# A decoder stack in one program: mod vectors spread over more steps, a first block interleaved with its norm, and a second norm scale taken from block sums

## Time and profile before

| what | value |
|---|---|
| median of 3 runs (lowest to highest) | 1957.84 us (1957.07 to 1960.55) |
| profiled execution | 1955.04 us |
| its span | 1953.4 us |
| mean granted clock of TensorE | 0.983 |
| PE busy | 1845.5 us, 94% |
| DVE busy | 1427.5 us, 73% |
| ACT busy | 902.8 us, 46% |
| POOL busy | 118.3 us, 6% |
| transfers | 424.80 MB, mean 217 GB/s |

### The profile page before, as it was taken

One profiled execution on the slowest core, in us unless ns is written; L12 is line 12 of the kernel. 1 busy time (PEld: TensorE's weight loads), 2 busy tenths in 40 slices (PEclk: granted clock), 3 DMA queues, 4 the chain that ended last, 5 costly groups with the idle time before them and its releaser, 6 DMA issues.

```text
span 1953.4 us, 29752 instructions
## 1 busy us (share of the span) xinstructions
PE 1845.5 (94%) x11620; PEld 1664.0 (85%) x11620; DVE 1427.5 (73%) x1613; ACT 902.8 (46%) x1204; POOL 118.3 (6%) x217
## 2 busy tenths in 40 slices
PE   5999999999999999999999979998999997999997
PEld 5999978789889988988998767776888787999976
DVE  4699996777778887888788967643667666786754
ACT  4444456454434444444444465422556445444442
POOL 0100000001110000000000000000111000000000
PEclk9999999999999999999999989998999998999998
DMA  6855445858888787767877654544444583777652
GB/s 227 285 195 193 161 154 203 280 188 275 314 311 276 241 270 257 252 213 266 257 249 281 231 214 141 200 140 151 162 153 137 204 285 110 242 234 261 212 186 87
DMA packets 185319, 424.80 MB, mean 217 GB/s; under 512 B 8192, under 2 KB 8576, under 8 KB 183680
## 3 DMA queue, kind: packets, MB, share of 16 engines
q1 hardware_dynamic: 157568, 322.69, 48.4%
q0 software_dynamic: 27648, 100.68, 15.6%
HBM read 419.14 MB, written 4.19 MB: 217 GB/s over the span
## 4 chain that ended last, share of the span: by engine, by line
PE 72%; DVE 14%; DMA 6%; ACT 4%; issue 3%; SPq 0%; POOLq 0%; DVEq 0%; ACTq 0%; POOL 0%
PE acc L1622 11%; PE acc L1623 11%; PE acc L1624 11%; PE acc L1609 11%; PE acc L1611 11%; PE acc L1610 11%; DVE w_lo L956 4%; DMA mod_raw<-in_od_mod_w 3%; DMA mod_raw<-in_ev_mod_w 2%; DVE mod_sum L995 2%; DVE mod_sum L1118 2%; PE aux L1658 2%; PE aux L1870 1%; ACT w_hi L482 1%; DVE scratch L1244 1%
## 5 line engine op out<-in xcount | busy, mean ns | idle before, releaser
L482 ACT ACTIVATE w_hi<-raw 128x1024 fp32r<-128x1024 f32 x552 | 575.4, 1057 | 673.1 <-PE acc L1611 331.5
L956 DVE TENSOR_TENSOR w_lo<-raw,w_hi 128x1024 fp32r<-128x1024 f32 x552 | 665.3, 1223 | 273.7 <-ACT w_hi L482 272.7
L1609 PE MATMUL acc<-a_hi,w_hi 128*128 128x256 f32 x2304 | 659.3, 286 | 15.4 <-DVE w_lo L956 15.1
L1611 PE MATMUL acc<-a_hi,w_lo 128*128 128x256 f32 x2304 | 653.0, 283 | 0.0
L1610 PE MATMUL acc<-a_lo,w_hi 128*128 128x256 f32 x2304 | 652.9, 283 | 0.0
L1609 PEld LDWEIGHTS acc<-a_hi,w_hi 128*128 128x128 f32 x2304 | 443.4, 192 | 18.1 <-DVE w_lo L956 9.8
L1610 PEld LDWEIGHTS acc<-a_lo,w_hi 128*128 128x128 f32 x2304 | 443.4, 192 | 0.5 <-issue 0.4
L1611 PEld LDWEIGHTS acc<-a_hi,w_lo 128*128 128x128 f32 x2304 | 443.1, 192 | 0.0
L995 DVE SCALAR_TENSOR_TENSOR mod_sum<-mod_raw,silu_c,mod_sum 128x1024 f32<-128x1024 f32 x240 | 301.6, 1279 | 46.9 <-DMA mod_raw<-in_ev_mod_w 25.5
L1622 PE MATMUL acc<-w_hi,b_hi 128*128 128x512 f32 x800 | 314.7, 393 | 7.3 <-DVE w_lo L956 7.3
L1623 PE MATMUL acc<-w_lo,b_hi 128*128 128x512 f32 x800 | 312.4, 391 | 0.0
(11 more groups left out here) (200 smaller groups left out, 1394.1 us busy)
## 6 DMA issues: line engine op xcount, KB each, us to landing
raw<-in_w_ff SPq DMA_DIRECT2D x128, 1024.0 KB, 6.7
mod_raw<-in_ev_mod_w POOLq DMA_DIRECT2D x96, 512.0 KB, 4.9
mod_raw<-in_od_mod_w POOLq DMA_DIRECT2D x96, 512.0 KB, 5.1
raw<-in_w_in SPq DMA_DIRECT2D x40, 1024.0 KB, 5.1
raw<-in_ev_w_in SPq DMA_DIRECT2D x40, 1024.0 KB, 5.2
raw<-in_od_w_in SPq DMA_DIRECT2D x32, 1024.0 KB, 5.4
raw<-in_w_out SPq DMA_DIRECT2D x16, 1024.0 KB, 5.3
raw<-in_ev_w_out SPq DMA_DIRECT2D x16, 1024.0 KB, 6.5
```

The costliest lines, as they stand in the source:

```text
L482: nc.scalar.activation(w_hi[:, s % SLOTS], raw[:, s // 2, KPS * (s % 2):KPS * (s % 2) + KPS, :], ACT.Copy).then_inc(hi_ready, 1)
L956: nc.vector.tensor_tensor(w_lo[:, s % SLOTS], raw[:, s // 2, KPS * (s % 2):KPS * (s % 2) + KPS, :], w_hi[:, s % SLOTS].bitcast(F32), ALU.s ...
L1609: nc.tensor.matmul(o, wh, hi[:, k, :], start=first and t == 0 and f % 2 == 0, stop=False, skip_group_check=True)
L1611: last = nc.tensor.matmul(o, wl, hi[:, k, :], start=False, stop=t == KPS - 1, skip_group_check=True)
```

## The change

Four new small tensors hold the partial sums. The rest, by place:

- **First block.** The order becomes pair, split, pair, split for pairs and splits 4 to 7. The convolution's input is cleared in its padding only. `neg_sink` is moved ahead of the first scale, and the root's table is loaded before x is there. ACT's loop over the first four blocks is unrolled.
- **Mod vectors.** The 12 halves that stood beside the first two blocks (six to a block) now stand 4 beside the first splits of block 1 and 8, two to a pair of splits, beside the rest. Three more halves of `ev_gate` move from the feed-forward to the w_out product. In the feed-forward nothing is done for p under 6, units of two vectors go at 5/12 a step, and a turn is done one part at a time, in four of five steps. Two halves of `od_scale` go from the end of the feed-forward to `evq` and `evkv`.
- **Feed-forward.** ACT's sums of squares are left out in the first three groups.
- **Last two boundaries.** The sum of squares of x + r*y is taken as xx + 2r*xy + r*r*yy. xx is the sum that the norm before left; yy (ACT) and xy (DVE) are summed by block while the product still runs. s is found before most of x is updated, and the additions follow between the pairs.
- **Context.** SP no longer waits for `ssq_ready` before it loads the context.

```diff
@@ ACT and DVE, first block (ACT's calls; DVE has the same with lo)
-            norm_scaled(0, col("g_mix_pre", 0, KT), a_hi, range(4, 8))
+            norm_scaled(0, gain, a_hi, [4])
+            split_hi(0, [4])
...
+            norm_scaled(0, gain, a_hi, [7])
+            split_hi(0, [7])
@@ DVE
-            link(nc.vector.memset(conv_in, 0.0))
+            link(nc.vector.memset(conv_in[:, :, 0:PAD], 0.0))
...
-                run_ahead(b, three("ev_gate", 0) if i == 0 else lambda m: conv_taps(7 + m % 2))
-                run_ahead(b + 1, three("ev_gate", 3) if i == 0 else lambda m: conv_taps(7 + m % 2))
+                if i == 0:
+                    split_lo(b + 1, (0, 1))
+                    halves("ev_gate", 0, 2)
+                    split_lo(b + 1, (2, 3))
+                    halves("ev_gate", 2, 2)
+                else:
+                    run_ahead(b, lambda m: conv_taps(7 + m % 2))
+                run_ahead(b + 1, each("ev_gate", 4, (2, 2, 2, 2)) if i == 0 else lambda m: conv_taps(7 + m % 2))
@@ DVE, feed-forward
+                def turn(unit, part, sums_before, temp, p, start):
+                    first, count = spread(p, start, 4, 5, 0, 4 * MOD_VECTORS[unit])
+                    if count:
+                        turn_parts(unit, first // 4, part + first // 4, sums_before, temp, first % 4, count)
...
+                    if 6 <= p < 18:
+                        halves("ev_gate", *spread(p, 6, 5, 8, 25, 32))
+                    elif 18 <= p < 23:
+                        turn("ev_gate", 1, 0, ff_temp, p, 18)
+                    elif 23 <= p < 75:
+                        halves("od_shift", *spread(p, 23, 5, 8, 0, 32))
+                    elif 75 <= p < 80:
+                        turn("od_shift", 0, 0, ff_temp, p, 75)
+                    elif 80 <= p < 157:
+                        halves("ev_shift", *spread(p, 80, 5, 12, 0, 32))
+                    elif 157 <= p < 167:
+                        turn("ev_shift", 0, 1, ff_temp, p, 157)
+                    elif 167 <= p < 244:
+                        halves("ev_scale", *spread(p, 167, 5, 12, 0, 32))
+                    elif 244 <= p < 254:
+                        turn("ev_scale", 0, 2, raw_temp, p, 244)
@@ DVE, boundaries
+            def gained_products(i):
+                for tt in range(TT):
+                    part = slice(BW * i, BW * (i + 1))
+                    link(nc.vector.scalar_tensor_tensor(xy_junk, Y[:, tt, part], 1.0, X[:, tt, part], ALU.mult, ALU.mult,
+                                                        accum_out=xy_part[:, tt, i:i + 1]))
+
+            def residual_sums(n, squares, meanwhile):
+                dve.wait_ge(yy_done, squares)
+                xx, yy, xy, t = (sums[:, i, :] for i in range(4))
+                nc.vector.tensor_reduce(yy, yy_part[:], AX.X, ALU.add)
+                link(nc.vector.tensor_reduce(xy, xy_part[:], AX.X, ALU.add))
+                link(nc.vector.tensor_tensor(t, yy, resid_s[:], ALU.mult))
+                link(nc.vector.scalar_tensor_tensor(t, xy, 2.0, t, ALU.mult, ALU.add))
+                link(nc.vector.tensor_tensor(t, t, resid_s[:], ALU.mult))
+                link(nc.vector.tensor_tensor(xx, xx, t, ALU.add))
+                mean_eps(n, xx, norm_s[:, 6:8], meanwhile)
+                token_diagonals()
...
+                last_add(n)
+                dve.wait_ge(ff_tile, TT * (n + 1))
+                dve.sem_inc(acc_free, 1)
...
                 if n:
                     ff_gained(n - 1)
+                    dve.wait_ge(gained_tile, TT * n)
+                    gained_products(n - 1)
+            ff_gained(NBLK - 1)
...
-            add_to_residual(range(3))
-            split_lo(BLOCK["evq"], (2, 3))
-            add_to_residual([3])
...
-            residual_scale(4, 18)
+            post_scale(3, products_and_scales)
+            residual_sums(4, TT * NBLK, lambda: add_to_residual([0]))
@@ DVE, first_pairs
-                pair_modulated(m, scale, shift, a_hi, a_lo, range(4))
+                add_to_residual([1])
+                pairs(0)
+                add_to_residual([2])
+                pairs(1)
+                split_lo(block, [2])
+                add_to_residual([3])
+                pairs(2)
+                split_lo(block, [3])
+                pairs(3)
@@ SP
-            sp.wait_ge(ssq_ready, 18)
```

More of the change, by code:

```diff
@@ L1040, in mean_eps @@
                 dve.wait_ge(std_ready, n + 1)
-                link(nc.vector.reciprocal(norm_s[:, 6:8], norm_s[:, 4:6]))
+                link(nc.vector.reciprocal(result, norm_s[:, 4:6]))
             def token_diagonals():
@@ L1201, in _ @@
             ahead1(34)
-            halves("ev_gate", 13, 1)
+            halves("ev_gate", 13, 2)
             ahead1(35)
@@ L1216, in _, with gained @@
                     ahead1({0: 37, 2: 38, 5: 39}[k])
-            def gained(squares, i, source):
+            def gained(squares, i, source, each_tile=None):
                 for tt in range(TT):
@@ L1230, in _ @@
                     if f % 2:
-                        halves("ev_gate", 14 + 2 * i + f % 4 // 2, 1)
+                        halves("ev_gate", 15 + 2 * i + f % 4 // 2, 1)
                 gained(2 * i, i, out_acc[i])
@@ L1234, in _ @@
                 ahead1(f)
-                if f in (52, 54):
-                    halves("ev_gate", 20 + (f - 52) // 2, 1)
+                if f < 56:
+                    halves("ev_gate", 21 + f - 52, 1)
             gained(6, 3, out_acc[3])
@@ L1275, in _, with spread @@
             split_lo(BLOCK["ff"], (6, 7))
-            def spread(unit, p, start, num, den, first=0, last=2 * KT):
+            def spread(p, start, num, den, first, last):
                 done = lambda q: min(max(first + (q - start) * num // den, first), last)
-                halves(unit, done(p), done(p + 1) - done(p))
+                return done(p), done(p + 1) - done(p)
             def ff_mods(n):
+                def turn(unit, part, sums_before, temp, p, start):
+                    first, count = spread(p, start, 4, 5, 0, 4 * MOD_VECTORS[unit])
+                    if count:
+                        turn_parts(unit, first // 4, part + first // 4, sums_before, temp, first % 4, count)
@@ L1408, in _ @@
                 else:
-                    run_ahead(BLOCK["evq"] + n, each("od_scale", 2, (1, 1, 1, 0)) if n == 3 else None)
+                    run_ahead(BLOCK["evq"] + n, each("od_scale", 0, (1, 1, 1, 1)) if n == 3 else None)
                 norm_modulated(3, b_hi, b_lo, ctx_tiles[n])
@@ L1416, in _ @@
                 n = 4 + m
-                run_ahead(BLOCK["evkv"] + m, each("od_scale", 5 + 5 * m, (1, 1, 1, 2) if m == 0 else (1, 2, 1, 2)))
+                run_ahead(BLOCK["evkv"] + m, each("od_scale", 4 + 6 * m, (1, 2, 1, 2)))
                 dve.wait_ge(acc_free, 2 + ACC["evkv"] + 2 * (m + 1))
```

209 lines of the change are left out of this document (123 added, 86 removed).

## The result

The changed kernel takes 1929.71 us (median of four runs, 1927.82 to 1932.13), the kernel before 1958.76 in the same comparison (median of four, 1957.07 to 1960.55): ratio 0.9852, interval 0.9835 to 0.9869. The forecast was 1933 with a range of 1923 to 1944. The profiled execution takes 1930.26 us with a span of 1928.6, which is 24.8 us less than the span of before, the very sum of the prediction. That the two agree to a tenth is luck. It compares one execution of each kernel, and that of the kernel before was a quick one (1955.04 us). Between the medians lie 29.05 us, and the interval stands for 25.7 to 32.3.

The account below looks back on a forecast made before the run. PE, busy for 1845.5 us, was taken to bound the kernel, so only its waits and low clock could be won. -8.7 + 3.8 + 0.4 - 15.1 - 2.2 - 3.0 = -24.8 us from 1957.84 gave 1933, range 1923 to 1944.

Parts of the forecast that it names:

- First block: First block: PE's wait of 6.26 us and 2.7 us of low clock go, neg_sink costs 0.2; -8.7 us.
- Mod chain: Mod halves beside block 1: load rounds of 7.85 us make PE wait longer at block 2; +3.8 us.
- rival 1: Mod halves beside block 1: the loads keep up with PE, total -30.7 us, 1927; chance 0.17.
- Other mod halves: Around the first convolution tile: DVE may wait for half 14 of ev_gate; +0.4 us, bounds 0 and 1.5.
- the 0.4 for the last group: Feed-forward's last group: more work at block ends costs +0.4 us, bounds 0 and 2.
- Feed-forward: Feed-forward: all eight w_lo waits, 14.0 us, and 1.5 us of low clock go, +0.4 for the last group; -15.1 us.
- Rivals 4 and 5: Feed-forward: DVE cannot hold 5/12, slower, chance 0.03; or stalls only move, 12 us less gained, 1945, chance 0.04.
- Boundary into evq: Boundary into evq: DVE's chain takes 11.5 us for 14.1, accumulators cost +0.4; -2.2 us.
- Rival 2: Last two boundaries: they gain nothing, for instance with products at half rate; 5.2 us less gained, 1938, chance 0.15.
- Spill and context: After the feed-forward: the context behind SP's later spill still comes about when ACT wants it; nothing, bounds 0 and 4 us.
- Boundary into odu: Boundary into odu: the chain takes 9.4 us with hand-overs for 12.8, +0.4 for accumulators; -3.0 us.
- The clock: First block and near 870 us: low clock after the removed gaps goes, 2.7 and 1.5 us, counted within those terms.

Follow-up runs that it names:

- The three parts: The kernel before with only the first block, only the feed-forward or only the boundaries changed: 1952.93, 1941.55 and 1953.81 us.

## Why the prediction was right, step by step

**First block, -8.7.** The wait went (6.26 of 6.26), and the start of the span gained 0.3 where 0.2 was to be lost. The low clock at its place went too, but the part alone is worth 6.3 us timed, so its 2.7 us cannot be seen in the time.

**Mod chain, +3.8.** Measured +0.6. This was the step named as least sure, and of the waits it is the term that was mis-sized most. The start was right: the second pair was used at 52.76 for 52.8 predicted. The rounds were not. The landings of these twelve loads, with 5.9 taken from the earlier trace rows:

```profile
DMA to landing us min/median/max: 4.5/5.2/6.7
```

Four rounds from 52.76 to 80.76 make 7.0 us each for 7.85, of which the median landing explains 0.7. Over the profiles this holds: the twelve loads have medians of 5.5 to 6.4 us in the four kernels that start as before, and of 4.8 to 5.5 in the nine with this start and twelve halves. The gate is at 83.21 for 86.6 and PE waits 2.75 for 5.9. So it came out between the main case and rival 1. The Trainium skill ("DMA: Bandwidth & Descriptors", the anatomy of one DMA) would have the load at 3.2 us; the quickest here took 4.5, and the trace still does not agree.

**Other mod halves, +0.4,** and the 0.4 for the last group: neither shows as a wait. Zero was in the bounds of both. No run shows either cost.

**Feed-forward, -15.1.** The waits went whole (14.0 of 14.0), the forecast's mechanism held at 5/12, and its bound was tested from above: 5/8 fails. My reason was too broad in one thing: turns of four parts cost nothing at positions 20 and 77, so there they need not be cut up. The low clock near 870 us went, and the part alone saved some 3 us more than its waits, so here its 1.5 us may well be in the time. Rivals 4 and 5 fall.

**Boundary into evq, -2.2.** Measured -3.02 in the wait. The chain of DVE after, from the last addition to the diagonals; the bracket of the first row is the wait for PE's block:

```profile
1105.88 1.29 DVE L1435 TENSOR_TENSOR scratch<-scratch,acc 128x512 f32<-128x512 f32 x2 [1.25 <-PE acc L1728]
...
1111.60 0.68 DVE L1325 SCALAR_TENSOR_TENSOR scratch<-scratch 128x512 f32<-128x512 f32 x1
1112.21 0.08 DVE L1325 DVE_READ_ACCUMULATOR scratch<-scratch 128x1 f32 x1
...
1113.06 0.26 DVE L1072 TENSOR_TENSOR mod_cols<-aux,cols 128x16 f32<-128x16 f32 x2
...
1116.61 0.48 DVE L1087 TENSOR_SCALAR ln_rstd<-ident,norm_s 128x128 f32<-128x128 f32 x2
```

From 1105.88 to 1116.61 it takes 10.7 us; the prediction had 10.9 to there and 0.4 for the accumulators. A pair of products with its accumulators takes 1.46 us (1111.60 to 1113.06) for 1.6 in the prediction, and the small instructions overlap a little. The 0.8 is made of such small terms.

**Half rate.** The Trainium skill ("Vector Engine (DVE) Microarchitecture Reference", "Points that are easy to get wrong") has a scalar-tensor-tensor with two non-bf16 SBUF sources at half rate. The trace does not agree: with an accumulator it takes 0.69 us for 128x512, the price of a plain one. Rival 2 falls, and doubling the products (1.46 us for two) says it in PE's time.

**Spill and context, 0.** Measured +1.6. The term stayed inside its bounds (0 and 4), but the step failed, because it had no margin. I had the context at about 1164 and ACT's want at 1166.2 - 2.3 = 1163.9, on a scale on which the product ends where it did before. On that scale, 23.67 us behind the span of after, the spill was issued at 1151.0 (1151.5 predicted) and the context landed at 1164.7: it took 13.0 us behind the spill, for 12.0 before. ACT stood from 1162.6, earlier than 1163.9. Loading the context ahead of the spill removes the wait; it then landed in 8.9 and 9.7 us in the two profiles.

**Boundary into odu, -3.0.** Measured -3.67, by the same small terms.

**The clock, -4.2 in all.** Between the two profiles +0.5; in the timed runs, 3.7 us more than the waits were saved. The low clock of the earlier trace rows was charged to the gaps that went, and it went there. In the profile of after low clock stands at other short waits, and by it that profile loses what the prediction had counted; but such stretches stand in profiles of kernels without the whole change as well. How loosely it is tied to a kernel shows in the page's first line of two more profiles of the same changed kernel, beside the one above:

```profile
PE 1846.2 (96%) x11620; PEld 1666.2 (86%) x11620; DVE 1439.2 (75%) x1663; ACT 884.8 (46%) x1153; POOL 118.3 (6%) x217
```
```profile
PE 1842.6 (96%) x11620; PEld 1662.9 (86%) x11620; DVE 1438.7 (75%) x1663; ACT 885.2 (46%) x1153; POOL 118.7 (6%) x217
```

The three differ by up to 3.6 us of PE's busy time with the same work, nearly as much as the term. The three comparisons of the changed kernel saved 29.05, 26.7 and 30.2 us between medians, against 25.3, 24.4 and 26.1 us of waits in their profiles: 2 to 4 us more each time. The three parts, timed alone, give no such order: the feed-forward saved more than its waits, the other two less. So whether the 4.2 us were won is open. The estimate by medians leans on the waits of a single profile of the kernel before, and they vary: its feed-forward has 14.0 us of waits for `w_lo`, the three kernels with the old placing of these halves have 11.2 to 11.5.

**The sum.** Without its clock the prediction had -20.6 us of waits, and -25.3 were measured. The mod chain was 3.2 us better than its term, the boundaries 1.5, the start of the span 0.5 and the two small terms 0.8; the context was 1.6 worse, and 0.3 is not placed. With the clock at +0.5 this makes the -24.8 of the two profiles, a chance agreement; the medians of the timed runs lie 4.2 us beyond it. The mechanisms held, except for the context's margin, and the sizes that were off are the mod chain's most of all. What decides after which short waits the clock falls was not tried and stays open.

## What to carry to other kernels

Where an engine beside the bound one is far from full and PE still waits for it, look for lumps: parts of a periodic job that stand in one place. Ten microseconds in two neighbouring positions cost 3.5 to 4.5 each time here, five cost 0 to 1.2, and cut up both cost nothing. A gap at a boundary that is one engine's serial chain can be added up from its durations and moved by putting off whatever the next engine does not need first; after such a move look at every queue that waits for the piece put off, here the context behind the spill. Do not judge what the clock gives back by one profile of each kernel: three executions of one kernel differed by 3.6 us of PE's busy time here, where 4.2 were sought. And when a sum is met to a tenth, compare its terms one by one, and the medians, before believing it.

## What was not expected of the hardware

- The granted clock: behind the same two waits of 2.5 us of the same kernel it was 0.62 to 0.63 in two executions and 1.00 in a third. Over the profiles of all these kernels, with the same matmuls, PE was busy for 1842.6 to 1855.8 us.
- DVE's accumulator after a scalar-tensor-tensor costs 0.08 us, where ACT's read costs 0.19.
- A load of 512 KB from POOL's queue landed in 5.2 us in the median with twelve of them closer together than before, when the median was 5.9. The other profiles bear it out (4.8 to 5.5 for 5.5 to 6.4); why, no run shows.
